# A mixture-of-experts block on one Trainium2 core: last stage moved into both branches, a shorter activation, part of the last stage on GpSimd, and another point where the weight loads change order

## What is computed

```python
h = rms_norm(x, moe_norm)                    # 32 experts, 4 per token
gu = h[tokens of e] @ w_up[e] + b_up[e]      # 1024 -> 2 x 1024
x_glu, x_lin = split(gu); x_glu = min(x_glu, 7); x_lin = clip(x_lin, -7, 7)
act = x_glu * sigmoid(1.702 * x_glu) * (x_lin + 1)
x = x + gate * (act @ w_down[e] + b_down[e])
h = rms_norm(x, ple_norm)
x = x + sigmoid(h @ ple_gate_w) * (p @ ple_proj_w)
return rms_norm(x, final_norm)
```

## Time and profile before

| | |
|---|---|
| median of 3 runs | 1177.22 us (1176.24 to 1178.27) |
| the profiled execution | 1176.2 us |
| its span, by the profile | 1174.5 us |
| TensorE busy | 1115.2 us (95%) |
| VectorE busy | 443.4 us (38%) |
| ScalarE busy | 241.7 us (21%) |
| GpSimd busy | 10.5 us (1%) |
| HBM read | 446.05 MB, 381 GB/s over the span |
| granted clock, mean | 0.99 |

### The profile page before, as it was taken

The page is one execution under the profiler, slowest core; times in us unless marked ns, Lnnn a source line. Parts: engine busy times, 40 slices in busy tenths (PEclk is TensorE's granted clock), DMA queues, the critical chain, the costliest instruction groups (busy, mean ns, idle before and its releaser), DMA issues.

```text
span 1174.5 us, 14590 instructions
## 1 busy us (share of the span) xinstructions
PE 1115.2 (95%) x5847; PEld 532.4 (45%) x5847; DVE 443.4 (38%) x732; ACT 241.7 (21%) x327; POOL 10.5 (1%) x29
## 2 busy tenths in 40 slices
PE   8999999899999999999999899999999999999987
PEld 8999998433333333333333333333333333333336
DVE  5899896722232222121212122222222222222246
ACT  5455452311111111111111011111111111111136
POOL 2000000000000000000000000000000000000000
PEclk9999999999999999999999999999999999999999
DMA  9864568999999999999999999999999999999981
GB/s 307 300 215 146 182 256 292 387 417 429 428 428 427 429 428 429 429 429 429 429 429 428 429 407 412 429 429 429 429 429 429 429 429 427 428 427 427 425 325 37
DMA packets 58559, 447.63 MB, mean 381 GB/s; under 512 B 4131, under 2 KB 26907, under 8 KB 33723
## 3 DMA queue, kind: packets, MB, share of 16 engines
q1 hardware_dynamic: 57380, 443.65, 91.4%
q0 software_dynamic: 672, 1.99, 0.5%
q10 hardware_dynamic: 471, 1.47, 0.4%
HBM read 446.05 MB, written 1.05 MB: 381 GB/s over the span
## 4 chain that ended last, share of the span: by engine, by line
PE 54%; DMA 32%; DVE 9%; ACT 3%; issue 1%; SPq 1%; POOL 0%; DVEq 0%; POOLq 0%; ACTq 0%
PE ps L1706 19%; DMA down_ring<-in_expert_w_down_dram 17%; DMA up_ring<-in_expert_w_up_dram 15%; PE ps L1745 14%; PE ps L1519 6%; PE ps L1529 3%; PE ps L1758 2%; DVE work L1317 2%; PE ps L1865 2%; PE ps L1603 1%; DVE w_lo L433 1%; DVE work L1305 1%; DVE work L1301 1%; PE ps L1735 1%; DVE work L1302 1%
## 5 line engine op out<-in xcount | busy, mean ns | idle before, releaser
L1706 PE MATMUL ps<-up_ring,hT 128*64 128x512 f32 x2048 | 449.2, 593 | 9.6 <-DMA up_ring<-in_expert_w_up_dram 8.6
L1706 PEld LDWEIGHTS ps<-up_ring,hT 128*64 128x64 f32 x2048 | 149.0, 137 | 301.5 <-issue 278.9
L1745 PE MATMUL ps<-down_ring,hT 128*64 128x512 f32 x992 | 232.8, 612 | 23.7 <-DMA down_ring<-in_expert_w_down_dram 16.7
L1301 DVE TENSOR_SCALAR work<-ps 128x512 f32<-128x512 f32 x32 | 22.1, 692 | 492.8 <-PE ps L1717 492.8
L1745 PEld LDWEIGHTS ps<-down_ring,hT 128*64 128x64 f32 x992 | 68.6, 140 | 164.4 <-issue 143.5
L1287 DVE TENSOR_TENSOR x_sb<-x_sb,ps 128x1024 f32<-128x1024 f32 x64 | 77.8, 1215 | 169.3 <-PE ps L1758 163.8
L829 ACT ACTIVATE work<-work 128x512 f32<-128x512 f32 x31 | 19.5, 630 | 397.5 <-DVE work L1301 397.5
L674 ACT ACTIVATE w_hi<-up_ring 128x2048 fp32r<-128x2048 f32 x31 | 59.2, 1914 | 77.9 <-PE ps L1529 44.2
L1519 PE MATMUL ps<-h_hi,w_hi 128*128 128x256 f32 x304 | 74.2, 284 | 0.0
L1519 PE MATMUL ps<-h_lo,w_hi 128*128 128x256 f32 x304 | 73.7, 283 | 0.0
L433 DVE TENSOR_TENSOR w_lo<-up_ring,w_hi 128x2048 fp32r<-128x2048 f32 x32 | 72.9, 2284 | 2.0 <-ACT w_hi L674 1.0
(11 more groups left out here) (265 smaller groups left out, 833.9 us busy)
## 6 DMA issues: line engine op xcount, KB each, us to landing
up_ring<-in_expert_w_up_dram SPq DMA_DIRECT2D x127, 2048.0 KB, 26.1
down_ring<-in_expert_w_down_dram SPq DMA_DIRECT2D x64, 2048.0 KB, 21.6
up_ring<-in_w_in_dram SPq DMA_DIRECT2D x21, 1024.0 KB, 5.5
up_ring<-in_branch_w_dram SPq DMA_DIRECT2D x6, 1024.0 KB, 4.9
up_ring<-in_w_out_dram SPq DMA_DIRECT2D x4, 1024.0 KB, 6.0
up_ring<-in_ple_gate_w_dram SPq DMA_DIRECT2D x4, 1024.0 KB, 26.5
up_ring<-in_expert_w_up_dram SPq DMA_DIRECT2D x2, 1024.0 KB, 38.2
x_sb<-in_x_dram SPq DMA_DIRECT2D x2, 512.0 KB, 4.1
```

The source lines that it names most:

```text
L1301: nc.vector.tensor_scalar(glu, ps[:, GLU, :], LIMIT, None, ALU.min).then_inc(glu_ready, 1)
L1706: ins = nc.tensor.matmul(ps[64 * g:64 * g + 64, GLU + side, :], xe[:, j, k % 4, k // 4, :], w[:, D * side + 512 * g:D * side + 512 * (g + 1)],
L1745: last = nc.tensor.matmul(ps[64 * g:64 * g + 64, Y, :], actT[:, r, c, :], down_units[:, c, D * r + 512 * g:D * r + 512 * (g + 1)], start=( ...
```

## The change

- SyncE: for experts 18 to 21 the first up unit is loaded before the down units of the expert before, and the other three after them; the order up(q), down(q) begins at expert 22.
- GpSimd: adds 1 to the lin half of the up bias before ScalarE rounds it; takes the low parts of weight pieces 0 and 1; multiplies tiles 0 to 3 by the final gain.
- Activation: the lin half comes with its 1 and is clamped to -6 and 8; the sigmoid is taken straight from PSUM and clamped in the last product; the glu clamp is part of the product. `glu_ready` is gone. TensorE's next `up` waits for `prod_ready` in place of `lin_ready`.
- Last expert on TensorE: the early `to_tokens` comes ahead of the third up unit, and eight idle transposes stand behind `weight_columns`.
- Last stage, now inside both branches on ScalarE, VectorE and TensorE: token tile 0 is added and transposed in halves, its `h_hi` is taken before tile 1 is added; the `w_lo` pass of tiles 0 and 1 comes ahead of all of tiles 2 to 4; the squares of tiles 3 and 4 are taken on VectorE; the last step is a product with the reciprocal alone.

The diff, cut to its core:

```diff
+SIG_MAX = 1.0 / (1.0 + math.exp(-ALPHA * LIMIT))
@@ sync: load order @@
             refill_up(e + 1, 1, e + 1, range(DOWN_UNITS, UP_UNITS))
-            refill_down(e + 1, e + 1)
-            with sp.Fori(EARLY_LOADS // 2 + 1, N_EXP // 2 - 1) as i:
+            for q in range(e + 1, e + 5):
+                refill_up(q + 1, (q + 1) % 2, q + 1, [0])
+                refill_down(q, q)
+                refill_up(q + 1, (q + 1) % 2, q + 1, range(1, UP_UNITS))
+            refill_down(e + 5, e + 5)
+            with sp.Fori(EARLY_LOADS // 2 + 3, N_EXP // 2 - 1) as i:
@@ gpsimd @@
+            pool.wait_ge(bup_loaded, 16 * BIAS_PARTS)
+            nc.gpsimd.tensor_scalar(b_rest[0:BIAS_PARTS * N_EXP, D:2 * D], b_rest[0:BIAS_PARTS * N_EXP, D:2 * D],
+                                    1.0, None, ALU.add).then_inc(b_shifted, 1)
+            for m in range(2):
+                pool.wait_ge(g_hi_ready, m + 1)
+                gate_lo_part(nc.gpsimd, m).then_inc(g_lo_ready[m], 1)
+            pool.wait_ge(gain_loaded, 16)
+            for i in range(4):
+                a, at, n = FINAL[i]
+                cols = slice(at, at + n)
+                pool.wait_ge(ple_x_ready, i + 1)
+                nc.gpsimd.tensor_tensor(final_out[:, a, cols], x_sb[:, a, cols], final_gain[:, cols], ALU.mult
+                                        ).then_inc(scaled_ready, 1)
@@ scalar @@
-            act.wait_ge(bup_loaded, 16 * BIAS_PARTS)
+            act.wait_ge(b_shifted, 1)
...
-                act.wait_ge(glu_ready, q + 1)
+                act.wait_ge(up_done, q + 1)
                 wait_past(act, prod_ready, 2 * q)
-                nc.scalar.activation(sig, glu, ACT.Sigmoid, scale=ALPHA).then_inc(sig_ready, 1)
+                nc.scalar.activation(sig, ps[:, GLU, :], ACT.Sigmoid, scale=ALPHA).then_inc(sig_ready, 1)
...
+            def tile_squares(i):
+                act.wait_ge(ple_x_ready, i + 1)
+                own(nc.scalar.activation(xs[:, a, at:at + n], x_sb[:, a, at:at + n], ACT.Square,
+                                         accum_out=part_ssq[:, i:i + 1]))
+            def mean_square(i, out, so_far):
+                own(nc.scalar.activation(mean_sq[:, out:out + 1], part_ssq[:, i:i + 1], ACT.Identity,
+                                         bias=so_far, scale=1.0 / D))
+            def final_root(a, i, so_far):
+                nc.scalar.activation(rms[:, a:a + 1], part_ssq[:, i:i + 1], ACT.Sqrt, bias=so_far,
+                                     scale=1.0 / D).then_inc(final_rms, 1)
+            def last_stage():
+                for m in range(4):
+                    split_gate(m)
+                act.wait_ge(x_final, 1)
+                act.dma_start(final_gain, on_all(final_norm)).then_inc(gain_loaded, 16)
+                act.wait_ge(xfT_done, 3)
...
+                for a in range(TT):
+                    act.wait_ge(x_final, a + 2)
+                    square_sum(a)
+                root().then_inc(rms_ready, 1)
+                nc.scalar.activation(small[:, 34:35], eps, ACT.Sigmoid)
+                act.wait_ge(rstd_ready, 2)
+                gate_sigmoid(0)
+                gate_sigmoid(1)
+                tile_squares(0)
+                mean_square(0, 0, eps)
+                tile_squares(1)
+                final_root(0, 1, mean_sq[:, 0:1])
+                nc.scalar.activation(small[:, 34:35], eps, ACT.Sigmoid)
+                gate_sigmoid(2)
+                gate_sigmoid(3)
+                tile_squares(2)
+                mean_square(2, 1, eps)
+                gate_sigmoid(4)
+                nc.scalar.activation(small[:, 34:35], eps, ACT.Sqrt)
+                act.wait_ge(ple_sq_ready, 1)
+                mean_square(3, 2, mean_sq[:, 1:2])
+                act.wait_ge(ple_sq_ready, 2)
+                final_root(1, 4, mean_sq[:, 2:3])
+            steps_so_far = steps[0]
             with act.If(overflow < 1):
                 last_expert(N_EXP - 1)
+                last_stage()
+            steps[0] = steps_so_far
@@ vector @@
             def gated_product(q):
                 dve.wait_ge(up_done, q + 1)
-                nc.vector.tensor_scalar(glu, ps[:, GLU, :], LIMIT, None, ALU.min).then_inc(glu_ready, 1)
-                nc.vector.tensor_scalar(lin, ps[:, LIN, :], LIMIT, -LIMIT, ALU.min, ALU.max).then_inc(lin_ready, 1)
-                dve.wait_ge(glu_ready, q + 1)
+                nc.vector.tensor_scalar(lin, ps[:, LIN, :], 1.0 + LIMIT, 1.0 - LIMIT, ALU.min, ALU.max
+                                        ).then_inc(lin_ready, 1)
                 dve.wait_ge(lin_ready, q + 1)
-                nc.vector.scalar_tensor_tensor(out=lin, in0=lin, scalar=1.0, in1=glu, op0=ALU.add,
+                dve.wait_ge(sig_ready, q + 1)
+                nc.vector.scalar_tensor_tensor(out=lin, in0=ps[:, GLU, :], scalar=LIMIT, in1=lin, op0=ALU.min,
                                                op1=ALU.mult).then_inc(prod_ready, 1)
                 dve.wait_ge(prod_ready, 2 * q + 1)
-                dve.wait_ge(sig_ready, q + 1)
...
-                nc.vector.tensor_tensor(act_cols, lin.rearrange("p (c r) -> p c r", r=DOWN_ROWS),
-                                        sig.rearrange("p (c r) -> p c r", r=DOWN_ROWS), ALU.mult).then_inc(prod_ready, 1)
+                nc.vector.scalar_tensor_tensor(out=act_cols, in0=sig.rearrange("p (c r) -> p c r", r=DOWN_ROWS),
+                                               scalar=SIG_MAX, in1=lin.rearrange("p (c r) -> p c r", r=DOWN_ROWS),
+                                               op0=ALU.min, op1=ALU.mult).then_inc(prod_ready, 1)
...
             def finish(q):
-                dve.wait_ge(comb_done, comb_before(q) + 1)
-                nc.vector.tensor_tensor(x_sb[:, 0, :], x_sb[:, 0, :],
-                                        ps[:, COMB:COMB + 2, :].rearrange("p a b -> p (a b)"),
-                                        ALU.add).then_inc(x_final, 1)
+                for h in range(2):
+                    cols = slice(512 * h, 512 * (h + 1))
+                    if h == 0:
+                        dve.wait_ge(comb_done, comb_before(q) + 1)
+                    nc.vector.tensor_tensor(x_sb[:, 0, cols], x_sb[:, 0, cols], ps[:, COMB + h, :],
+                                            ALU.add).then_inc(x_final, 1)
+                for k in range(KT):
+                    gain = ROW["ple_norm"] + k
+                    if k % 4 == 0:
+                        dve.wait_ge(xfT_done, k // 4 + 1)
+                    nc.vector.tensor_scalar(h_hi[:, k, 0:P], final_columns(0, k), prm[:, gain:gain + 1], None,
+                                            ALU.mult).then_inc(xf_hi_ready[0], 1)
                 dve.wait_ge(comb_done, comb_before(q) + 2)
                 nc.vector.tensor_tensor(x_sb[:, 1, :], x_sb[:, 1, :],
                                         ps[:, WT:WT + 2, :].rearrange("p a b -> p (a b)"),
                                         ALU.add).then_inc(x_final, 1)
...
+            def tile_squares(i):
+                a, at, n = FINAL[i]
+                dve.wait_ge(ple_x_ready, i + 1)
+                nc.vector.scalar_tensor_tensor(out=squares_out[:, 0:n], in0=x_sb[:, a, at:at + n], scalar=1.0,
+                                               in1=x_sb[:, a, at:at + n], op0=ALU.mult, op1=ALU.mult,
+                                               accum_out=part_ssq[:, i:i + 1]).then_inc(ple_sq_ready, 1)
             def final_norm_of(a):
                 dve.wait_ge(final_rms, a + 1)
                 own(nc.vector.reciprocal(frstd[:, a:a + 1], rms[:, a:a + 1]))
+                dve.wait_ge(scaled_ready, (2, 5)[a])
                 for h in range(2):
                     cols = slice(h * 512, (h + 1) * 512)
-                    nc.vector.scalar_tensor_tensor(out=final_out[:, a, cols], in0=x_sb[:, a, cols],
-                                                   scalar=frstd[:, a:a + 1], in1=final_gain[:, cols],
-                                                   op0=ALU.mult, op1=ALU.mult).then_inc(final_ready, 1)
-            dve.wait_ge(ple_proj_ready, PROJ_PARTS)
-            gated_x(0)
-            gated_x(1)
-            dve.wait_ge(gain_loaded, 16)
-            gated_x(2)
-            final_norm_of(0)
-            gated_x(3)
-            gated_x(4)
-            final_norm_of(1)
+                    nc.vector.tensor_scalar(final_out[:, a, cols], final_out[:, a, cols], frstd[:, a:a + 1], None,
+                                            ALU.mult).then_inc(final_ready, 1)
+            def last_stage(q):
+                finish(q)
+                final_low_parts(0)
+                for m in range(2, 4):
+                    split_gate(m)
+                dve.wait_ge(rms_ready, 2)
+                nc.vector.reciprocal(rstd, rms).then_inc(rstd_ready, 1)
+                final_low_parts(1)
+                dve.wait_ge(ple_proj_ready, PROJ_PARTS)
+                gated_x(0)
+                gated_x(1)
+                final_norm_of(0)
+                gated_x(2)
```

(51 more changed lines are left out.)

126 lines of the change are left out of this document (42 added, 84 removed).

## The result

The kernel before takes 1178.27 us (median of 5 runs, 1176.24 to 1179.5), the changed one **1170.95 us** (5 runs, 1170.76 to 1172.97): ratio 0.9946, interval 0.9931 to 0.9960. In a second comparison of the same pair (6 runs against 17) it is 1169.65 to 1178.32, 0.993 [0.9906, 0.9953]. So it is faster, by 7.3 and 8.7 us where 10.5 was forecast, and the first median is inside the range only by its upper edge.

The account below looks back on a forecast made before the run. The HBM weight stream was taken as the bound until about 1114 us, then expert 31's path to the last store. A -2.65, B -2.85, C -1.95, D -0.6, E -2.5 sum to -10.55 us: 1166.7 us, range 1164.0 to 1171.0.

Parts of the forecast that it names:

- A, load order: Load queue after 681.9 us: one more queued up unit fills the traffic gap at 700 to 715 us; -2.65 us.
- No new gap: Load stream over the next four experts: each step has 2 us more queued, so the whole -2.65 us is gained.
- gap stays: Rival: the load-order switch again drains the queue somewhere; 1169.3 us, chance 0.12.
- B, last expert: Expert 31, from the third up unit to tile 0's result: filled wait, shorter activation, held clock; -2.85 us.
- in the 31 other experts this is hidden by the stream: Activation's dropped VectorE step: -0.6 us in expert 31, no effect on the time in the other experts.
- my -1.6 for the clock: Expert 31's down product: idle transposes hold TensorE's clock, which had fallen to 0.66; -1.6 us, bounds 0 and -1.7.
- C, to the first gate pass: From TensorE's result of tile 0 (T0) to the first gate pass: T0 + 3.94 becomes T0 + 2.0; -1.95 us.
- D, the gate passes: Gate passes fed without a gap, ending (E) at T0 + 25.5 against T0 + 28.06; -0.6 us besides the part before.
- E, the end: From the end of TensorE's last gate pass (E) to the span's end, 8.6 us before; -2.5 us, bounds -1.8 and -2.9.
- GpSimd slows VectorE: Rival: GpSimd's gain products double VectorE's products of tiles 3 and 4, +1.7 us; 1168.5 us, chance 0.14.
- x E + 1.5 ... reciprocal E + 2.85: After the last gate pass: x done 1.5 us behind its end, the reciprocal 2.85 us behind.
- E + 3.65, end at E + 6.1: After the last gate pass: scalings done 3.65 us behind its end, the span's end 6.1 us behind.

Follow-up runs that it names:

- the first pair: First profiled executions of the kernel before (1176.2 us) and of the changed kernel (1172.1 us).
- the second pair: Second traces of the kernel before (1173.6 us) and of the changed kernel, both unaltered; the gains in span sum to 4.2 us.
- experiment 4: The changed kernel with the load order of before alone put back: 1172.57 us, ratio 0.9955 to the kernel before.
- experiment 5: The kernel before with the new load order alone: 1177.99 us, ratio 0.9996 to the kernel before.
- experiment 10: The changed kernel with the last stage behind the branches again on TensorE, ScalarE and VectorE: 1175.56 us, ratio 0.9986 to the kernel before.
- experiment 7: The changed kernel with all four low parts of the gate weights on VectorE again: 1173.62 us, ratio 0.9965 to the kernel before.
- the first batch: Experiments 1 to 4, run with their own runs of the kernel before (median 1178.32 us); the unaltered changed kernel took 1169.65 us there.

## Why the prediction was right and wrong

**A, load order (-2.65): the step "No new gap" failed.** The gap at 702 closed as worked out. But the order met a gap some 20 us earlier, at expert 15's down product, which I had taken as fed: its wait of 4.76 us, and the half product of 5.11 us behind it, were in the trace of before and not read. With it A is worth -2.1 us in the first pair and -0.7 in the second (426 against 417 and 423 against 420 GB/s over 640 to 740 us). It is needed in the changed kernel (experiment 4), yet alone it is worth nothing that the runs can tell (5). The rival "gap stays" was half right.

**B, last expert (-2.85): right for expert 31 where the clock would have fallen, wrong in "in the 31 other experts this is hidden by the stream".** From the third up unit to T0 it gained 3.1 and 1.5 us; the difference is the clock, which was up in the second and third trace of before. Of my -1.6 for the clock, the cost is there in two of four traces without the idle transposes (the first of before, and experiment 5), and in none of the ten with them. As an average it is about half of what I wrote. Hidden is also true only where nothing else waits: at expert 0 the table load moved onto the path, and the stream lost about 0.8 us. Of the 2.5 us by which the third up unit starts later in the first pair, 1.1 are in the issue of its load already, after a head that was slower at 205 to 235 us too (the up product at a fallen clock). The other 1.4 are a longer time to landing (median of these loads 36.6 us against 35.2), which I can't explain.

**C, to the first gate pass (-1.95): right where it was put, but the exit was priced from one row.** T0 + 1.84 against a forecast T0 + 2.0. I gave the exit of the branch 1.2 us, counted from the end of the first add. Counted so, the three traces of before show 1.2, 2.3 and 1.9, and experiment 10 shows 3.7, with 1.4 us of fallen clock behind it. As a price of the branch move in the changed kernel 1.2 us is refuted by the 4.9 us of experiment 10. In the three traces of the kernel before the first gate pass starts at T0 + 3.94, 5.05 and 4.62, yet E is at T0 + 28.1, 28.3 and 27.9: the first trace lost 0.8 us in its gate passes, 0.60 of it in one stall, that the other two did not.

**D, the gate passes (-0.6): the time of E right, the share of D partly luck.** E at T0 + 25.43, forecast T0 + 25.5. From the first gate pass to E the first pair gains 0.5 us (24.1 to 23.6), but the second loses 0.4 (23.3 to 23.6): only the sum of C and D holds, and experiment 7 shows that it hangs on GpSimd's low parts. Their 4.6 us each lay under the bound of 6.4. The Trainium skill, "GPSIMD Engine Reference", section "Performance versus the Vector engine", has 4497 ns for a two-input add of 2048 float32 elements, not for a product as the prediction calls it. The low part is a subtraction of that size, and the trace's 4.6 us agree.

**E, the end (-2.5): the step that failed alike in both pairs; -0.8 and -0.9.** Two terms of it. "x E + 1.5 ... reciprocal E + 2.85" holds only without GpSimd's products; beside them it is E + 3.78, so the rival "GpSimd slows VectorE" is real, at 0.95 us instead of 1.7. Its price was worked out wrongly: the VectorE operation does not double, it takes what is left of GpSimd's and then about its own time. The Trainium skill, "GPSIMD Engine Reference", section "Key points", says that the two share their SBUF interfaces, with contention at VectorE instructions with two SBUF inputs; the rows agree. I gave it a chance of 0.14. "E + 3.65, end at E + 6.1" carried over 2.45 us from the last scaling to the end; it was 3.15, with 0.6 of the difference in the landing of the last stores. That is another 0.7.

**The sum.** Of the 6.4 us that the first pair of traces lacks, 5.1 are the stream's and 1.7 the end's, less 0.3 gained more by B and 0.1 by C and D. In the second pair 3.6 are the stream's, 1.6 the end's and 1.4 B's (the clock that had not fallen), less 0.3 by C and D. By the stretches above, the first 5.1 are 1.7 of fallen clock at expert 0, 1.4 of landing, 0.8 of expert 0's activation, 0.6 that A fell short, and 0.6 that no stretch explains. The second 3.6 are 1.9 that A fell short, 1.0 at expert 0, and 0.7 unexplained.

The medians differ by 7.3 and 8.7 us where the traces differ by 4. The executions that were profiled of the kernel before took 1176.2, 1173.6 and 1177.15, among runs that reach 1183.16; the runs of the changed kernel stay within 1168.7 to 1173. Two things that vary in the kernel before are settled by the change, the clock of B and the length of the branch exit, and may be part of that spread. Each run's mean granted clock is on record and bears on it: among the 17 runs of before in the first batch the fastest (1174.06 us) has 0.993 and the slowest (1183.16) 0.984, and time and clock go together almost run by run, by about 0.9 us for each 0.001. The changed kernel's six runs beside them have 0.9905 in the mean and these 17 have 0.9882, so some 2 of the 8.7 us between the medians go with the clock (an estimate from these runs). From 0.993 to 0.984 is more than the one fall at expert 31, which costs 1.7 us. No trace covers the longest runs of before, so where else their clock falls stays open.

## What to carry to other kernels

Before you call a shortened step hidden, look at its first use: a table load or a cold start puts it on the path there. Before you move work to GpSimd, ask what two-input VectorE work stands beside it, and on whose path; here two early low parts were worth 2.6 us in the trace (3.6 to 4.0 in the medians), late products with the gain cost 0.95. And straight-line work behind a branch is worth moving into the branch when the engines that leave it are the ones that set the end. Last, take two parts that feed one wait as one term: here C's 2 us were gone again as soon as the low parts were late.
